# A two-block transformer on one core: seven of the 31 depthwise taps of the convolution as products with diagonals on TensorE

## The reference

```python
def conformer_conv(h, pw1_w, pw1_b, dw_w, dw_b, ln_g, ln_b, pw2_w, pw2_b):
    a = h @ pw1_w + pw1_b
    u, g = jnp.split(a, 2, axis=-1)
    u = u * jax.nn.sigmoid(g)
    u = lax.conv_general_dilated(
        u, dw_w[:, None, :].astype(u.dtype), window_strides=(1,),
        padding=[(CONV_PAD, CONV_PAD)], dimension_numbers=("NWC", "WIO", "NWC"),
        feature_group_count=D_MODEL) + dw_b
    ...
    return jax.nn.silu(u) @ pw2_w + pw2_b
```

## Time and profile before

| | us |
|---|---|
| median of 3 runs (3715.48 to 3720.54) | 3717.98 |
| span of the profiled execution | 3701.0 |
| median less that span | 17.0 |
| TensorE busy in the span | 3428.7 |
| VectorE busy | 1652.7 |
| ScalarE busy | 1252.2 |
| GpSimd busy | 2.6 |

### The profile page before, as it was taken

One profiled execution on the slowest core, in us unless ns is written; L12 is line 12 of the kernel. 1 busy time (PEld: TensorE's weight loads), 2 busy tenths in 40 slices (PEclk: granted clock), 3 DMA queues, 4 the chain that ended last, 5 costly groups with the idle time before them and its releaser, 6 DMA issues.

```text
span 3701.0 us, 52884 instructions
## 1 busy us (share of the span) xinstructions
PE 3428.7 (93%) x18622; PEld 2778.8 (75%) x18622; DVE 1652.7 (45%) x3040; ACT 1252.2 (34%) x2502; POOL 2.6 (0%) x7
## 2 busy tenths in 40 slices
PE   8999989989999989979999777889998999799998
PEld 8976769969985779848888343568885888666898
DVE  5544345545543255433223798442334233443555
ACT  4443134444442144433222311342224222421443
POOL 0000000000000000000000000000000000000000
PEclk9999589999997599989999998999998999875799
DMA  7555036455553045443322433333232332210253
GB/s 250 172 170 171 0 106 188 151 179 180 151 174 125 0 149 184 157 148 114 102 80 80 122 105 106 104 121 91 85 97 88 95 92 90 75 51 1 90 183 106
DMA packets 238209, 437.94 MB, mean 118 GB/s; under 512 B 26320, under 2 KB 27344, under 8 KB 237904
## 3 DMA queue, kind: packets, MB, share of 16 engines
q1 hardware_dynamic: 237344, 432.92, 37.4%
q0 software_dynamic: 688, 2.62, 0.2%
HBM read 434.39 MB, written 1.05 MB: 118 GB/s over the span
## 4 chain that ended last, share of the span: by engine, by line
PE 87%; DVE 8%; ACT 3%; issue 1%; DMA 0%; SPq 0%; DVEq 0%; ACTq 0%; POOL 0%
PE ps L627 84%; DVE ps L1388 4%; PE ps L932 2%; ACT zh L1043 1%; ACT hidden L1043 1%; DVE low L1385 1%; DVE std L1474 1%; DVE hidden L1385 1%; DVE hidden L1388 0%; DMA raw<-weights 0%; DVE x L1388 0%; ACT x L1043 0%; PE ps L952 0%; PE ps L716 0%; DVE zl L1385 0%
## 5 line engine op out<-in xcount | busy, mean ns | idle before, releaser
L627 PE MATMUL ps<-zh,low 128*128 128x256 f32 (+1 forms) x3680 | 1205.3, 328 | 168.1 <-DVE low L1385 118.3
L627 PE MATMUL ps<-zl,high 128*128 128x256 f32 (+1 forms) x3680 | 1195.9, 325 | 0.0
L627 PE MATMUL ps<-zh,high 128*128 128x256 f32 (+1 forms) x3680 | 1195.1, 325 | 0.0
L627 PEld LDWEIGHTS ps<-zh,low 128*128 128x128 f32 x3680 | 717.3, 195 | 252.7 <-DVE low L1385 121.8
L1385 DVE TENSOR_TENSOR low<-raw,high 128x512 fp32r<-128x512 f32 x1304 | 828.5, 687 | 165.4 <-ACT high L1043 147.5
L1043 ACT ACTIVATE high<-raw 128x512 fp32r<-128x512 f32 x1304 | 729.0, 621 | 157.8 <-PE ps L627 88.2
L627 PEld LDWEIGHTS ps<-zh,high 128*128 128x128 f32 x3680 | 717.0, 195 | 52.5
L627 PEld LDWEIGHTS ps<-zl,high 128*128 128x128 f32 x3680 | 718.2, 195 | 49.9
L627 PE MATMUL ps<-h_split,high 128*128 128x256 f32 (+1 forms) x2816 | 644.2, 324 | 0.0
L627 PEld LDWEIGHTS ps<-h_split,high 128*128 128x128 f32 x2816 | 474.3, 191 | 41.6
L627 PE MATMUL ps<-h_split,low 128*128 128x256 f32 (+1 forms) x1408 | 456.3, 324 | 15.4 <-DVE h_split L1385 13.9
(11 more groups left out here) (150 smaller groups left out, 1799.4 us busy)
## 6 DMA issues: line engine op xcount, KB each, us to landing
raw<-weights SPq DMA_DIRECT2D x1640, 256.0 KB, 3.0
cst<-consts SPq DMA_DIRECT2D x1, 1808.0 KB, 13.7
x<-x_in SPq DMA_DIRECT2D x1, 1024.0 KB, 7.2
x<-ctx_in POOLq DMA_DIRECT2D x1, 1024.0 KB, 11.2
out<-hidden POOLq DMA_DIRECT2D x1, 1024.0 KB, 5.0
ple_p<-p_in POOLq DMA_DIRECT2D x1, 512.0 KB, 6.7
```

Of the source, the lines that this page charges most:

```text
L627: return nc.tensor.matmul(out, lhsT, rhs, start=first, stop=last, **kw)
```

## The change

Taps 0 to 6 and the bias of each channel tile are done on TensorE. GpSimd multiplies the identity with the tap's 128 weights, giving eight 128x128 diagonals per tile (`taps_full`: seven taps and the bias), ScalarE copies them as fp32r (`taps_h`) and GpSimd subtracts (`taps_l`); the tile's input is split in the same manner (`cin_h` by ScalarE, `cin_l` by GpSimd). `diagonal_taps(m)` makes two products for the bias (against ones) and three for each tap, 23 in all, into the PSUM accumulator of tile m. VectorE waits for them (`conv_pe`) and adds the remaining 24 taps. All loops now run to `KT + 1`, with the taps of tile n-1 in round n; `conv_high` of ScalarE does the tile before in the same way.

```diff
@@ class PE, conv
-                for n in range(KT):
-                    if n >= 2:
-                        pe.wait_ge(conv_taken, seen.now(conv_taken) + n - 1)
-                    for g in range(2):
-                        self.tile(ps[:, 2 * (n % 2) + g, :], 512, coming=coming if n == 0 and g == 0 else None)
-                    self.fill(6, 7)
+                for n in range(KT + 1):
+                    if n < KT:
+                        if n >= 2:
+                            pe.wait_ge(conv_taken, seen.now(conv_taken) + n - 1)
+                        for g in range(2):
+                            self.tile(ps[:, 2 * (n % 2) + g, :], 512, coming=coming if n == 0 and g == 0 else None)
+                        self.fill(6, 7)
+                    if n >= 1:
+                        self.diagonal_taps(n - 1)
...
+            def diagonal_taps(self, m):
+
+                pe = self.pe
+                acc = ps[:, 4 + m % 2, :].rearrange("p (a s) -> p a s", a=2)
+                pe.wait_ge(taps_low, m + 1)
+                pe.wait_ge(cin_low, m + 1)
+                if m >= 2:
+                    pe.wait_ge(z_ready, self.seen.now(z_ready) + m - 1)
+                ones = ones_r[:].unsqueeze(1).broadcast_to([P, S, 2])
+                self.mm(ps[:, 4 + m % 2, :], r(taps_l[:, PE_TAPS, :]), r(ones), True, False)
+                self.mm(ps[:, 4 + m % 2, :], r(taps_h[:, PE_TAPS, :]), r(ones), False, False)
+                for t in range(PE_TAPS):
+                    hi, lo = cin_h[:, :, t:t + S], cin_l[:, :, t:t + S]
+                    self.mm(acc, r(taps_l[:, t, :]), r(hi), False, False)
+                    self.mm(acc, r(taps_h[:, t, :]), r(lo), False, False)
+                    i = self.mm(acc, r(taps_h[:, t, :]), r(hi), False, t == PE_TAPS - 1)
+                i.then_inc(conv_pe, 1)
@@ class Act, conv
                     self.ahead(4)
                     self.take_rows()
+                    if n >= 1:
+                        self.conv_high(n - 1)
                     self.used(4)
...
+            def conv_high(self, m):
+
+                act = self.act
+                if m == 0:
+                    self.f(r(ones_r[:]), c("ones"), ACT.Copy)
+                else:
+                    act.wait_ge(conv_pe, m)
+                act.wait_ge(conv_taken, m + 1)
+                self.f(r(cin_h[:]), conv_in[:, m], ACT.Copy).then_inc(cin_high, 1)
+                act.wait_ge(taps_made, m + 1)
+                self.f(r(taps_h), taps_full, ACT.Copy).then_inc(taps_high, 1)
@@ class Dve, conv: the taps, now those of tile m = n - 1 behind the gate product of tile n
-                    self.link(self.ts(acc, conv_in[:, n, :, 0:S], w[:, n, 0:1], c("conv_b")[:, n:n + 1], ALU.mult, ALU.add))
-                    for t in range(1, TAPS):
...
-                        if t in (4, 10, 16, 22) and n < KT - 1:
-                            self.low_of_next_tile()
+                    if n >= 1:
+                        m = n - 1
+                        acc = ps[:, 4 + m % 2, :].rearrange("p (a s) -> p a s", a=2)
+                        v.wait_ge(conv_pe, m + 1)
+                        for t in range(PE_TAPS, TAPS):
...
+                            if t - PE_TAPS in (3, 8, 13, 18) and n < KT - 1:
+                                self.low_of_next_tile()
@@ GpSimd
+            for n in range(KT):
+                pool.wait_ge(conv_taken, n + 1)
+                if n:
+                    pool.wait_ge(taps_low, n)
+                w = c("conv_pe")[:, n * (PE_TAPS + 1):(n + 1) * (PE_TAPS + 1)].unsqueeze(2).broadcast_to([P, PE_TAPS + 1, P])
+                nc.gpsimd.tensor_tensor(taps_full, c("ident").unsqueeze(1).broadcast_to([P, PE_TAPS + 1, P]), w, ALU.mult).then_inc(taps_made, 1)
+                pool.wait_ge(cin_high, n + 1)
+                nc.gpsimd.tensor_tensor(r(cin_l[:]), conv_in[:, n], cin_h[:], ALU.subtract).then_inc(cin_low, 1)
+                pool.wait_ge(taps_high, n + 1)
+                nc.gpsimd.tensor_tensor(r(taps_l), taps_full, taps_h, ALU.subtract).then_inc(taps_low, 1)
```

More of the change, by code:

```diff
@@ L48 @@
 NMOD = 9
+PE_TAPS = 7
 PITCH = 32
@@ L68, in columns @@
               ("cmp_add", ST * NC), ("cmp_mul", ST * NC), ("kc_cos", NC), ("kc_sin", NC),
-              ("eps", 4), ("csil", KT * 2), ("final_g", KT), ("sink", 16), ("conv_w", KT * TAPS),
+              ("eps", 4), ("csil", KT * 2), ("final_g", KT), ("sink", 16), ("conv_w", KT * TAPS), ("ones", 2), ("conv_pe", KT * (PE_TAPS + 1)),
               ("conv_b", KT), ("conv_ln_g", KT), ("conv_ln_b", KT), ("pw1_b", 2 * KT), ("pw2_b", KT)]
@@ L130, in lay_constants @@
     put("conv_w", inp["conv_dw_w_2"][0].reshape(TAPS, KT, P).transpose(2, 1, 0).reshape(P, KT * TAPS))
+    put("ones", 1.0)
+    put("conv_pe", np.concatenate([inp["conv_dw_w_2"][0][:PE_TAPS], inp["conv_dw_b_2"][0][None]], 0)
+        .reshape(PE_TAPS + 1, KT, P).transpose(2, 1, 0).reshape(P, KT * (PE_TAPS + 1)))
     put("conv_b", cols(inp["conv_dw_b_2"][0]))
@@ L365, in build @@
         cmp_s = sb("cmp_s", [P, 8])
+        cin_h = sb("cin_h", [P, 2, S + 2 * PAD])
+        cin_l = sb("cin_l", [P, 2, S + 2 * PAD])
+        ones_r = sb("ones_r", [P, 2])
         gates = sb("gates", [P, ST, 12])
@@ L401, in build @@
         conv_out = carve(KT * 2 * (S + 2 * PAD), KT, 512)
+        taps_h, taps_l = (carve_of(h_split[:].rearrange("p a b c -> p (a b c)"), 1024 * i, PE_TAPS + 1, P) for i in range(2))
+        taps_full = carve(KT * 2 * (S + 2 * PAD) + KT * 512, PE_TAPS + 1, P)
         q_at = carve(0, KT, S)
@@ L443, in build @@
         conv_taken = sem("conv_taken")
+        taps_made = sem("taps_made")
+        taps_high = sem("taps_high")
+        taps_low = sem("taps_low")
+        cin_high = sem("cin_high")
+        cin_low = sem("cin_low")
+        conv_pe = sem("conv_pe")
         gates_ready = sem("gates_ready")
@@ L1285, in conv @@
                     self.fill(6, 7)
+                self.ahead()
+                self.conv_high(KT - 1)
                 seen(conv_taken, KT)
@@ new lines, in conv @@
+                for n in range(KT + 1):
+                    if n < KT:
+                        self.used(4)
+                        v.wait_ge(sig_ready, seen(sig_ready))
+                        self.stt(conv_in[:, n, :, PAD:PAD + S], ps[:, 2 * (n % 2), :].rearrange("p (a s) -> p a s", a=2), c("pw1_b")[:, n:n + 1],
+                                 gated[:, n % 2, :].rearrange("p (a s) -> p a s", a=2), ALU.add, ALU.mult).then_inc(conv_taken, 1)
+                        v.wait_ge(conv_taken, seen(conv_taken))
+                        self.fill(6, 7)
+                    if n >= 1:
[3 more added lines that the diff above has]
+                        for t in range(PE_TAPS, TAPS):
+                            last = t == TAPS - 1
+                            dst = conv_out[:, m, :].rearrange("p (a s) -> p a s", a=2) if last else acc
+                            i = self.stt(dst, conv_in[:, m, :, t:t + S], w[:, m, t:t + 1], acc, ALU.mult, ALU.add)
+                            if last:
+                                i.then_inc(z_ready, 1)
+                            else:
+                                self.link(i)
+                            if t - PE_TAPS in (3, 8, 13, 18) and n < KT - 1:
+                                self.low_of_next_tile()
@@ L1806, in _ @@
             pool.dma_start(x[:, :, S:512], ctx_in).then_inc(rest_landed, 16)
+            pool.wait_ge(consts_landed, 16)
+            for n in range(KT):
[8 more added lines that the diff above has]
+                nc.gpsimd.tensor_tensor(r(taps_l), taps_full, taps_h, ALU.subtract).then_inc(taps_low, 1)
             pool.wait_ge(result_ready, 1)
```

## The result

The changed kernel takes 3776.9 us (median of 4 runs, 3773.5 to 3777.8) where the kernel before takes 3719.3 (3715.5 to 3721.8): a ratio of 1.015, 95% interval 1.0136 to 1.0165, 57.6 us slower. The forecast was 3771 us with a range of 3756 to 3792.

The account below looks back on a forecast made before the run. TensorE was taken to bound the kernel almost everywhere, VectorE at the taps. A start costing 29.6 us, six closed rounds of 34.0 and a last 37.9 put the end 52.8 us later: 3771 us, range 3756 to 3792.

Parts of the forecast that it names:

- to the fourth `low`: VectorE, from the start of the 24 taps to the start of the fourth low: 16.85 us.
- to the fill: From the start of the fourth low to TensorE's fill: 4.02 us at full clock, 5.64 at 1.2 GHz.
- the fill: TensorE, behind each tile's last quarter: eight fp32 products, 7.03 us a round.
- the diagonals: TensorE, behind the fill: 23 products a tile, 5.27 us and 0.17 for the last one's end, 5.44 us.
- From the first gate product to the first tap: Start of the convolution: first tap at 2112.2 us, costing 29.6 us in which VectorE has no tap to do.
- the last two tiles: End of the convolution, without lows: 48 taps of 0.79 us on VectorE, 37.9 us.
- last quarters at 1.2 GHz: TensorE ahead of the fill: three sevenths of 1.62 us added a round, making rounds of 34.0 us.
- rival 1: VectorE's low and GpSimd's subtraction get in each other's way: 0 to 21 us, 9 at f = 2, giving 3780; chance 0.33.
- The diagonals did not run at 1.2 GHz: Rival for TensorE's diagonals: products 0.427 us apart, 4.6 us more in seven rounds, +32, 3803 us; chance 0.07.
- GpSimd is no bound: Rival that GpSimd is the bound (f over 10): at f = 15 rounds of 48 us, about 3908 us; chance 0.03.
- Rival 4: Faster, VectorE stays the bound: diagonals run in TensorE's waits for the lows, rounds of 22.3 us, 3700 us; chance 0.05.
- The closed chain: Each round: VectorE's taps and lows, then TensorE's last quarter, fill and diagonals before the next taps, 34.0 us.

Follow-up runs that it names:

- e2: The changed kernel with the diagonals of tile n-1 in the middle of tile n, between its two halves: 3704.8 us.
- e1: The changed kernel with the diagonals of tile n-1 behind tile n but ahead of its fill: 3717.7 us.
- e5: The changed kernel with the four lows after taps 1, 4, 7 and 10 of the 24 in place of 4, 9, 14 and 19: 3733.7 us.
- e4: The changed kernel with three taps and the bias on TensorE in place of seven, 11 products a tile in place of 23: 3751.6 us.
- e3: The changed kernel with the lows after taps 6, 10, 14, 19 in place of 4, 9, 14, 19: 3767.8 us.
- e10: The kernel before, all 31 taps on VectorE, with the taps of tile n-1 behind the gate product of tile n: 3732.2 us.
- e6: The changed kernel with the diagonals in mid tile and the lows after taps 1, 4, 7 and 10: 3702.6 us.
- e9: e2 with eight more taps of the last channel tile on TensorE, 15 in all: 3696.8 us.

## Why the prediction was right

By its own steps, for the round: to the fourth `low` 16.85 us, measured 17.98, of which 1.14 is the meeting with GpSimd, so 16.84 without it; to the fill 4.02, measured 4.07; the fill 7.03, measured 6.96; the diagonals 5.44, measured 5.66 (the two bias products start 0.27 us apart and the others 0.234, not 0.229). From the first gate product to the first tap it was 30.4 us (2081.76 to 2112.2), measured 30.47 (2097.95 to 2128.42); the last two tiles 37.9, measured 37.8 (2336.36 to 2374.18). VectorE's wait was 11 us, measured 11.11.

Two terms were off, in opposite directions. I added 0.69 us a round for last quarters at 1.2 GHz; none was: the six rounds measure 34.63 to 34.68 us, all with the short way to the fill. The half clock (0.50) is there in each round, but in the first quarter, behind TensorE's wait of 5.2 us for the first `low`, and TensorE waits for the third `low` after it anyway. The first and the last quarter of one round (columns as in the earlier trace rows):

```profile
2133.50:2138.60 5.10, 5.04 (x12) 4.00 (x13) 4.92 (x7) 0.00 (x0) 0.00 (x0) 0.50 0.19 51
2147.00:2150.20 3.20, 3.06 (x13) 2.24 (x14) 3.06 (x6) 0.00 (x0) 0.00 (x0) 1.00 0.26 82
```

And I left rival 1 at 0.33 and out of the sum, though it came, 1.14 us in each of six rounds; at GpSimd's length (2.35 us against 1.22 on VectorE, f = 1.9) my sum for it gives 1.3. So it was not the scenario of the forecast that came but rival 1 without cold quarters, and it was luck that the two, +6.8 and -4.1 us, partly cancel. With the diagonals' 0.22 us and the small misses of the other pieces in six rounds (+1.2) they make the 3.9 us by which the stage is longer than my sum of 272.3 (276.2). The other 2.0 of the 5.9 us by which the median lies above the forecast are the kernel before, 3719.3 us now against the 3718.0 that I started from, and what two medians can't tell.

The span went wrong by more than the median: 3754 was forecast and 3771.7 measured. I had taken the 17.0 us between the median and the profiled span of the kernel before as what lies around a span. In the profiled execution of the change, 3773.5 us long, 1.8 us lie around it. In the kernel before the profile had simply reached the stage early, 16 us before the change's did. The forecast of the median stands all the same, since it rests on the difference in the stage.

The other rivals. The diagonals did not run at 1.2 GHz, as their spacing shows. GpSimd is no bound: 5.6 us busy in a round of 34.67, its operations 1.6 to 1.9 times as long as VectorE's, near the factor of about two that the Trainium skill gives (GPSIMD Engine Reference, Performance versus the Vector engine). Rival 4, the faster kernel, was a true statement about another program: e2 is that program, and its round of 24.4 us against my 22.3 shows what I had left out of it, that TensorE's own work is then the bound. The late start is in both.

The closed chain is shown from four sides: taking the fill out (e1), the way to the fourth `low` shorter (e5), fewer products (e4), and the first `low` quick (e3) each shortened the round by what it took from the chain, e5 by up to 0.9 us less where the first quarter ran at half clock.

## What to carry to other kernels

When work moves to an engine that the profile shows waiting, ask what stands ahead of it in that engine's queue, and what the first engine does for it in the meantime: here the idle 41 us were real, and 23 products a tile fitted in them in mid tile (11 us faster than before) but the kernel was 57 us slower when they stood behind the fill. Write down the way from one engine's start to its next start through the other; if that loop is longer than either engine's own work, shorten the loop (order, earlier hand-overs) before moving any work. Doing the taps one tile later costs the start once, 15 us in e10, and has to be earned back.

## What the runs showed of the hardware

- An elementwise operation of GpSimd with 1024 fp32 columns takes 1.90 us (product, inputs broadcast) and 2.35 us (subtraction). When one of its operations and a VectorE subtraction (both inputs in SBUF) meet, the one that starts first keeps its length and the other ends later. In the changed kernel GpSimd was first: its subtraction took 2.34 us and the `low` 1.83 in place of 0.69. In e1 the `low` was first: it took 0.69 and GpSimd's subtraction of the input 1.65 in place of 1.40. In e2 both happen in a row: the `low` starts inside the subtraction of the input, ends 0.55 us behind it (2153.60), and the next subtraction, begun meanwhile, takes 2.85 in place of 2.35:

```profile
2152.17 1.43 POOL L1871 TENSOR_TENSOR cin_l<-hidden,cin_h 128x572 fp32r<-128x572 f32 x1 [5.01 <-ACT cin_h L1081]
2153.02 1.13 DVE L1439 TENSOR_TENSOR low<-raw,high 128x512 fp32r<-128x512 f32 x1
2153.56 2.85 POOL L1873 TENSOR_TENSOR h_split<-hidden,h_split 128x1024 fp32r<-128x1024 f32 x1
```

- VectorE's taps, which read one tensor from SBUF and one from PSUM, stayed 0.79 us apart beside GpSimd's subtractions (the change, 2128.42 to 2131.59: four taps in 3.17 us).
- TensorE's granted clock was 0.50 (1.2 GHz) in the first quarter behind a wait of 5.2 us in each round of the change, products 0.427 us apart, and 1.00 in the last quarter, where they were 0.23 apart. In e6, where TensorE is busy throughout, it stayed at 1.00.
- The same program ahead of the stage reached it between 2081.8 and 2101.2 us in the profiles of this study, a spread as large as some of the effects; the stage's own length, against that of the kernel before, agreed with the medians within 2 us in eight of nine kernels, and within 3.4 in the ninth (e9).
